# A two-layer attention kernel: the scores of a head pair as two 64-row matmuls into two banks

## The reference, cut to what matters

```python
# layer A: differential attention, 6 pairs of heads (c = 0, 1), causal
s = einsum('bqhcd,bkhcd->bhcqk', qi, kf) * scale
s = where(kpos <= qpos, s, NEG)
p = softmax(s); w = p[:, :, 0] - lam * p[:, :, 1]
o = einsum('bhqk,bkhe->bqhe', w, vf)            # then an RMS norm
# both layers: attention to a memory of 256 tokens, 4 heads, no mask
# layer B: 12 heads; with 256 tokens it is plain causal attention in one block
# third block, first half: 8 heads that share one key and one value,
#   the 64 best keys of each query (mask), a bias by distance, softmax
# third block, second half: retention, 8 heads: (q k^T * decay) v, no softmax
```

## Time and profile before

| | us |
|---|---|
| runs before, lowest, median, highest | 988.36, 989.8, 990.0 |
| profiled execution, its own time | 988.6 |
| its span in the trace | 986.9 |
| TensorE busy | 947.6 (96%) |
| VectorE busy | 570.8 (58%) |
| ScalarE busy | 474.7 (48%) |
| GpSimd busy | 70.9 (7%) |

### The profile page before, as it was taken

The page is one execution under the profiler, slowest core; times in us unless marked ns, Lnnn a source line. Parts: engine busy times, 40 slices in busy tenths (PEclk is TensorE's granted clock), DMA queues, the critical chain, the costliest instruction groups (busy, mean ns, idle before and its releaser), DMA issues.

```text
span 986.9 us, 13015 instructions
## 1 busy us (share of the span) xinstructions
PE 947.6 (96%) x4630; PEld 789.8 (80%) x4630; DVE 570.8 (58%) x769; ACT 474.7 (48%) x699; POOL 70.9 (7%) x132
## 2 busy tenths in 40 slices
PE   5999989999999999899999999999897999999998
PEld 4788778888888887788888888888776888888887
DVE  3777756654555577453855545548887364544543
ACT  4766565534444365562744344446344454434341
POOL 2101120100000010001100000002133000000000
PEclk9999999999999999899999999999997999999999
DMA  8843234755555544221855556455422055656551
GB/s 286 290 138 129 87 105 134 254 190 176 199 178 172 169 166 133 86 86 44 272 178 199 180 179 199 138 174 184 155 91 76 27 165 187 200 174 194 187 170 43
DMA packets 95435, 157.77 MB, mean 160 GB/s; under 512 B 5928, under 2 KB 37624, under 8 KB 95392
## 3 DMA queue, kind: packets, MB, share of 16 engines
q1 hardware_dynamic: 93872, 155.09, 47.2%
q10 hardware_dynamic: 1488, 2.10, 0.7%
q0 software_dynamic: 32, 0.02, 0.0%
HBM read 156.12 MB, written 1.06 MB: 159 GB/s over the span
## 4 chain that ended last, share of the span: by engine, by line
PE 85%; DVE 6%; ACT 4%; POOL 2%; issue 2%; DMA 1%; SPq 0%; ACTq 0%; DVEq 0%; POOLq 0%
PE proj L1388 14%; PE proj L1390 13%; PE proj L1389 13%; PE outp L1388 6%; PE outp L1390 6%; PE outp L1389 6%; PE score L1388 5%; PE score L1390 5%; PE score L1389 5%; PE turn L1415 4%; PE score L1544 2%; PE outp L1589 2%; DVE wlo L1660 1%; ACT whi L1180 1%; ACT qk L1292 1%
## 5 line engine op out<-in xcount | busy, mean ns | idle before, releaser
L1660 DVE TENSOR_TENSOR wlo<-raw,whi 128x2048 fp32r<-128x2048 f32 x145 | 329.7, 2278 | 223.6 <-ACT whi L1186 147.9
L1388 PE MATMUL proj<-whi,set_hi 128*128 128x512 f32 (+1 forms) x656 | 262.5, 400 | 9.6 <-DVE wlo L1660 6.7
L1390 PE MATMUL proj<-whi,set_lo 128*128 128x512 f32 (+1 forms) x656 | 256.6, 391 | 0.0
L1389 PE MATMUL proj<-wlo,set_hi 128*128 128x512 f32 (+1 forms) x656 | 256.1, 390 | 0.0
L1186 ACT ACTIVATE whi<-raw 128x2048 fp32r<-128x2048 f32 x64 | 122.6, 1916 | 143.7 <-PE outp L1390 57.5
L1180 ACT ACTIVATE whi<-raw 128x2048 fp32r<-128x2048 f32 (+1 forms) x81 | 153.0, 1902 | 35.4 <-PE outp L1390 17.5
L1388 PEld LDWEIGHTS proj<-whi,set_hi 128*128 128x128 f32 x656 | 124.6, 190 | 35.1 <-issue 8.9
L1390 PEld LDWEIGHTS proj<-whi,set_lo 128*128 128x128 f32 x656 | 124.5, 190 | 26.4
L1389 PEld LDWEIGHTS proj<-wlo,set_hi 128*128 128x128 f32 x656 | 124.9, 190 | 23.8
L1388 PE MATMUL outp<-whi,set_hi 128*128 128x512 f32 x268 | 105.5, 394 | 0.1
L1390 PE MATMUL outp<-whi,set_lo 128*128 128x512 f32 x268 | 104.5, 390 | 0.0
(11 more groups left out here) (184 smaller groups left out, 931.4 us busy)
## 6 DMA issues: line engine op xcount, KB each, us to landing
raw<-in_a_w_up SPq DMA_DIRECT2D x32, 512.0 KB, 4.4
raw<-in_a_w_down SPq DMA_DIRECT2D x32, 512.0 KB, 4.4
raw<-in_b_w_up SPq DMA_DIRECT2D x32, 512.0 KB, 4.3
raw<-in_b_w_down SPq DMA_DIRECT2D x32, 512.0 KB, 4.4
raw<-in_w_gate SPq DMA_DIRECT2D x22, 512.0 KB, 4.0
raw<-in_w_up SPq DMA_DIRECT2D x22, 512.0 KB, 4.9
raw<-in_w_down SPq DMA_DIRECT2D x22, 512.0 KB, 3.8
raw<-in_a_w_in SPq DMA_DIRECT2D x20, 512.0 KB, 6.5
```

What stands on the lines that cost most here:

```text
L1388: pe.matmul(out_, hi, wh, start=start, stop=False)
L1389: pe.matmul(out_, hi, wl, start=False, stop=False)
L1390: return pe.matmul(out_, lo, wh, start=False, stop=stop)
L1660: dve.tensor_tensor(shaped(wlo, u), shaped(raw, u), shaped(whi, u), ALU.subtract).then_inc(lo_done, 1)
```

## The change

- Queries stay in pairs: `heads` goes, every `turn_heads` of queries uses `pairs`. The first memset on GpSimd covers blocks 8 to 11 only (for the index scores), the second is dropped, with one of the waits of ScalarE.
- Scores run over 64 partitions: head 0 on partitions 0 to 63 into bank `Sb[0]`, head 1 on 64 to 127 into `Sb[1]`. One step now has two items; item 0 lies at column 0 of both banks, item 1 behind it.
- The masks are written first. The causal mask becomes a block of three times 128 columns (triangle, zeros, triangle), one matmul of 384 columns for each bank. Bias and selection matmuls also come ahead of the scores.
- VectorE waits for both banks, takes both maxima; ScalarE waits for both items' maxima, then does the four exponentials. Both banks are freed together by the second item (`both_s`).
- Retention scores the same way, both `a` in one go.

```diff
...
+        cmask = sb("cmask", [P, 3, P], BF16)
...
-        headq = qk[:, 0:16, :].rearrange("p (b c) n -> p b c n", c=2)
...
+        pb = lambda n: ctx.enter_context(nc.psum_tensor(n, [P, 2, COLS], F32))
+        Pp, Tp, Sp, Op = pb("proj"), pb("turn"), pb("score"), pb("outp")
+        Pb, Tb, Sb, Ob = ([pair[:, i, :] for i in range(2)] for pair in (Pp, Tp, Sp, Op))
...
+        def both_s(release):
+
+            n = count.s
+            count.s += 2
+            f = [free["S", b] for b in range(2)]
+            free["S", 0] = free["S", 1] = release
+            return n, f
...
-            it.s, it.s_free = s_use((exp_done, it.exp + 1))
             ITEMS.append(it)
-            st = add("scores")
-            st.it = it
+            if len(ITEMS) % 2 == 0:
+                first = ITEMS[-2]
+                first.at, it.at = 0, first.n
+                st = add("scores")
+                st.items = [first, it]
+                st.s, st.s_free = both_s((exp_done, it.exp + 1))
             return it
...
-        qk_pieces = lambda a: heads(0, a, 2) + pairs(2, 16 + a, 2)
+        qk_pieces = lambda a: pairs(0, a, 2) + pairs(2, 16 + a, 2)
...
+                    for b in (0, 2):
+                        ins = pool.affine_select(out=cmask[:, b, :], in_=cmask[:, b, :], compare_op=ALU.is_ge, fill=NEG,
+                                                 base=0, pattern=[[-1, P]], channel_multiplier=1)
+                    ins.then_inc(consts_made, 1)
...
-                    pool.memset(qk[:, 0:16, :], 0.0).then_inc(heads_zeroed, 1)
+                    pool.memset(qk[:, 8:12, :], 0.0).then_inc(heads_zeroed, 1)
...
-                elif st.kind == "late_loads":
-                    pool.wait_ge(o_evac, st.o)
-                    pool.memset(qk[:, 0:16, :], 0.0).then_inc(heads_zeroed, 1)
...
+                    act.wait_ge(nmax_done, st.items[1].i + 1)
+                    for it in st.items:
...
+                        for c in range(2):
+                            dst = e[:, it.buf, c * it.n:(c + 1) * it.n]
+                            src = Sb[c][:, it.at:it.at + it.n]
+                            ins = act.activation(dst, src, ACT.Exp, bias=it.nm[:, c:c + 1], scale=SCALE,
+                                                 accum_out=it.rs[:, c:c + 1])
+                        ins.then_inc(exp_done, 1)
...
+                    if kind in ("diff", "causal"):
+                        for c in range(2):
+                            add_mask(c, Sb[c][:, 0:3 * P], identb[:], cmask[:, :, :].rearrange("p b n -> p (b n)"))
+                    for it in st.items:
+                        for c in range(2):
+                            S = Sb[c][:, it.at:it.at + it.n]
+                            if kind == "idx":
+
+                                c0 = P - P * it.t
+                                add_mask(c, S, flip[:], btoep[it.pair // 2][:, 2 * it.pair % 4 + c, c0:c0 + it.n])
+                                add_mask(c, S, identb[:], selmask[:, it.t, 0:it.n])
+                    for i, it in enumerate(st.items):
+                        for c in range(2):
+                            ins = pe.matmul(Sb[c][:, it.at:it.at + it.n], qk[HALF[c], it.q, tok(it.t)],
+                                            it.k[HALF[c], 0:it.n], start=not opened[c], stop=i == 1)
+                            opened[c] = True
+                            if i == 1:
+                                ins.then_inc(s_full, 1)
...
+                    for a in range(2):
                         for c in range(2):
+                            ins = pe.matmul(Sb[c][:, a * TOK:a * P + TOK], qk[HALF[c], 4 + st.p, tok(a)],
+                                            qk[HALF[c], Q_QB + st.p, a * P:TOK], start=a == 0, stop=a == 1)
+                            if a == 1:
+                                ins.then_inc(s_full, 1)
...
+                    dve.wait_ge(s_full, st.s + 2)
+                    for it in st.items:
+                        behind(dve.tensor_reduce(it.nm, Sp[:, :, it.at:it.at + it.n], AX_X, ALU.max))
+                        dve.tensor_scalar(it.nm, it.nm, -SCALE, None, ALU.mult)\
+                           .then_inc(nmax_done, 1)
...
+                    dve.wait_ge(s_full, st.s + 2)
+                    dve.wait_ge(*st.after)
+                    for a in range(2):
...
+                            dst, src = rt[:, a, o:o + n], Sb[c][:, a * TOK:a * TOK + n]
```

More of the change, by code:

```diff
@@ L359, in turn_heads @@
             return st.use
-        LOW, HIGH, ALL = slice(0, DH), slice(DH, P), slice(0, P)
+        HALF, ALL = [slice(0, DH), slice(DH, P)], slice(0, P)
         tok = lambda t: slice(t * P, (t + 1) * P)
@@ L535, in build @@
         d = [diff_item(0, 0), diff_item(0, 1)]
-        qm_use = turn_heads(zq[:, 0], [0, 1], heads(0, 6, 2), chunk_ready(ev.chunk))[-1]
+        qm_use = turn_heads(zq[:, 0], [0, 1], pairs(0, 6, 2), chunk_ready(ev.chunk))[-1]
         zfree[0] = qm_use + 1
@@ L709, in build @@
         m += [mem_item(1, 0, qm_use, mkB), mem_item(1, 1, qm_use, mkB)]
-        q_use = turn_heads(zq[:, 0], [0, 1, 2, 3], heads(0, 0, 4), rope_ready(r0_.rope))[-1]
+        q_use = turn_heads(zq[:, 0], [0, 1, 2, 3], pairs(0, 0, 4), rope_ready(r0_.rope))[-1]
         zfree[0] = q_use + 1
@@ L803, in retention_scores @@
             st = add("retention_scores")
-            st.p, st.use, st.banks, st.after = p, max(kb_use, qb_use), [], after
-            for a in range(2):
-                count.decayed += 1
-                st.banks.append(s_use((decayed, count.decayed)))
+            st.p, st.use, st.after = p, max(kb_use, qb_use), after
+            count.decayed += 2
+            st.s, st.s_free = both_s((decayed, count.decayed))
         def retention_out(p):
@@ L839, in build @@
         i1 = index_scores(1)
-        kb_use = turn_heads(zq[:, 1], [0, 1, 2, 3], heads(0, 4, 4), rope_ready(rk.rope))[-1]
+        kb_use = turn_heads(zq[:, 1], [0, 1, 2, 3], pairs(0, 4, 4), rope_ready(rk.rope))[-1]
         zfree[1] = kb_use + 1
@@ L881, in build @@
         tile(gb, 1, 0, xb)
-        qa_use = turn_heads(zq[:, 0], [0, 1, 2, 3], heads(0, 0, 4), lambda t: (qn_done, t + 1))[-1]
+        qa_use = turn_heads(zq[:, 0], [0, 1, 2, 3], pairs(0, 0, 4), lambda t: (qn_done, t + 1))[-1]
         zfree[0] = qa_use + 1
@@ L1534, in _ @@
                 elif st.kind == "scores":
-                    it = st.it
-                    wait_turned(it.need)
-                    wait(it.s_free)
-                    if it.kind == "idx":
-                        pe.wait_ge(sel_done, it.t + 1)
-                        pe.wait_ge(bias_landed, 32)
-                    S = Sb[it.s % 2]
-                    for c in range(2):
-                        o = c * it.n
-                        ins = pe.matmul(S[:, o:o + it.n], headq[:, it.q, c, tok(it.t)], it.k[:, 0:it.n],
-                                        start=True, stop=it.kind == "mem")
-                        if it.kind == "idx":
-                            c0 = P - P * it.t
-                            pe.matmul(S[:, o:o + it.n], flip[:], btoep[it.pair // 2][:, 2 * it.pair % 4 + c, c0:c0 + it.n],
-                                      start=False, stop=False)
-                            ins = pe.matmul(S[:, o:o + it.n], identb[:], selmask[:, it.t, 0:it.n],
-                                            start=False, stop=True)
-                        elif it.kind != "mem":
-                            ins = pe.matmul(S[:, o + it.n - P:o + it.n], identb[:], cmask[:], start=False, stop=True)
@@ L1555, in _, with add_mask @@
-                    ins.then_inc(s_full, 1)
+                    wait_turned(max(it.need for it in st.items))
+                    for c in range(2):
+                        wait(st.s_free[c])
+                    kind = st.items[0].kind
+                    if kind == "idx":
+                        pe.wait_ge(sel_done, st.items[0].t + 1)
+                        pe.wait_ge(bias_landed, 32)
+                    opened = [False, False]
+                    def add_mask(c, dst, lhs, rhs):
+                        pe.matmul(dst, lhs, rhs, start=not opened[c], stop=False)
+                        opened[c] = True
```

53 lines of the change are left out of this document (11 added, 42 removed).

## The result

| | us |
|---|---|
| before, median of 11 runs (lowest, highest) | 989.19 (988.05, 990.2) |
| after, median of 11 runs (lowest, highest) | 992.24 (990.41, 995.89) |
| ratio after to before, 95% interval | 1.0040 [1.0027, 1.0052] |
| profiled execution of after: its own time, its span | 995.89, 994.2 |

The kernel became 3 us slower. The profiled execution of after is the slowest of its eleven: 3.7 us above their median. Its trace therefore shows some of the loss larger than it usually is.

What follows compares the result with a forecast made beforehand. TensorE, busy 947.6 of 986.9 us, was taken as the bound, with latency counting in exposed steps. Gains of 3.3 us against delays of 7.1 made it net 3.8 us slower: 993.5 us, range 986 to 1000.

Steps and rivals of the forecast that it cites:

- the delays in my sum: Later hand-over in exposed diff, causal, last idx and retention steps: 7.1 us paid, 2.7 of it in three causal steps.
- my gains: Shorter TensorE parts in covered diff, mem, causal and idx steps, plus cheaper query copies: 3.3 us kept.
- the signs that I had named: Trace checks: idle time up 5 to 7 us, busy time down; wrong if clock-0.50 time changes by more than 3 us.
- The wait of the 434.49 kind: TensorE's wait before the second item's transposes in a causal step: to grow from 0.47 to 0.9 us.
- TensorE's part of a step: TensorE time per step: diff and causal 1.50 us, gain about 0.2; mem 1.37 us, gain 0.36.
- Five slots for eight passes: Score matmuls as two tiles overlap partly: 0.87 us against 1.30 in diff or causal steps, 1.08 against 1.73 in mem.
- Rival 1: Passes overlap to one half and changing tile size is free: 3.2 us faster, 986.6; 0.25, shared with a removed clock stretch.
- The change of tile size: Switching TensorE between 128-row and 64-row tiles costs 0.14 us a change, 0.29 in and out of a step.
- Latency of both items in one hand-over: In a causal step, first exponential at +3.0 us instead of +1.48, last transposes at +4.8 instead of +3.91.
- The copies: Full-height query copies save 7.7 us on ScalarE, mostly hidden; credited 0.8 at the third diff step, 0.25 before 396.97.
- rival 3: Half-clock stretches: one more costs about 2 us, one removed gains 3.4; no chance of its own, split between other cases.
- Where a product covers the hand-over: Steps with more TensorE work between scores and transposes than the delay: it costs nothing and the gain stays.

Runs made afterwards that it cites:

- the ladder: Four kernels compared: before with hand-over of both items 1006.99 us; after with full-height scores and half-height copies 1002.34; after with half-height copies 999.06; after 992.24.
- hand-over alone: Kernel before, with only VectorE waiting for both items' scores and ScalarE for both items' maxima: 1006.99 us, ratio 1.0189 to before.
- tiles in covered steps: Kernel before, with 64-row tiles, masks first and hand-over of both items only in steps that a whole weight product follows: 986.18 us, ratio 0.9974 to before.
- The fillers: Identity matmuls put into TensorE's waits: on the kernel after 990.09 us, ratio 1.0006 to before; on the kernel before 986.63 us, ratio 0.9977.

## Why the prediction was right, and which steps of it were wrong

The forecast was 993.5 us, slower; the median is 992.2, inside the range and on the forecast's side. The mechanism was the right one: the late hand-over costs more than the tiles give. That the sum came out is luck all the same. By the ladder, full-height scores and half-height copies with the late hand-over, masks first and the banks by head cost 13.3 us, where the delays in my sum were 7.1; tiles and copies then gave back 10.1, where my gains were 3.3. Two misses of 6 to 7 us cancelled.

Of the signs that I had named, some came out against me. The time at clock 0.50 changed by 27 us in the profiled execution, where more than 3 was to mean wrong. TensorE's busy time rose by 5.3 us, by the half clock, instead of falling, and its idle time grew by 2.0 us (39.3 to 41.3) and not by 5 to 7. The wait of the 434.49 kind stayed at 0.47 us and didn't grow to 0.9; the new one of 0.91 came as named. The transposes did come later, and the step stayed above 1.2 us.


- **TensorE's part of a step** was mis-sized. "Five slots for eight passes" assumed that a matmul of tile B can't start beside the first pass of tile A. The pairs start 6 to 7 ns apart, so it is four slots: a differential step takes 1.29 us instead of the 1.50 forecast, a memory step with its entry 1.15 instead of 1.37. Rival 1's full overlap was true. The Trainium skill (TensorE: Matmul & The Clock Gate, Part 3: Packing small matmuls — row/col tiling) has starts about 4 ns apart, and the trace agrees in kind with 6 to 7.
- **The change of tile size** was about right. The two masks start at 60.031 and 60.205 and the first tile pass at 60.460, so after a mask of 0.17 it comes 0.08 late, and this first pass lasts 0.21 us (to 60.674) where the next of the same width lasts 0.11. Behind the last pass, at 61.010, the next work starts 0.31 us later, of which the pass itself takes 0.21: 0.10, and its first transpose takes 0.05 more than those behind it (61.317, 61.481, 61.590). That is 0.18 in and 0.15 out, where I had 0.14 each way. Rival 1's free change didn't come.
- **Latency of both items in one hand-over** was right in the trace: first exponential +2.87 us (forecast +3.0), last transposes +4.64 (+4.8). The diff stretch cost +3.5 us with 3.4 at half clock in it (forecast +2.3), the product behind the idx steps waited 1.9 us for its score bank, where it had waited 0.40 at 775.79. Not foreseen was the rotation on VectorE behind the maxima, 1.16 us at 90.41.
- **The price of that hand-over as a whole** was far too low: 7.1 us of delays in my sum, where hand-over alone cost 18, and with masks first and the banks by head 13.
- **The copies** failed most clearly. I credited 1.05 us; half-height copies in after cost 6.8. By the ratios it is 5.2, and still five times my term. My step "Most of it is hidden beside products" was the wrong one: the copies cost spread over most stretches, 2.2 us before 115.85 without any half clock. The stretch of the second layer's query turns fell by 4.3 us, where I had 0.25, but that is for the most part not the copies: with half-height copies and tiles in covered steps it fell by 3.7. There the place of the half clock counts. That a shorter wait "may remove" the stretch of 6.8 us stood only among the rivals; it came halfway, since 3.4 us came back at 388.9.
- **The clock** was in my text only as rival 3, with "one more stretch of a few us, about 2 us" at 434 to 446. In the profiled execution that place held 13.6 us at half clock, and all of the trace 27 us more than before. The fillers put its part of the median at about 2 of 3 us, an estimate. A correct forecast should have carried it in every delay of an exposed step, not beside the sum.
- **Where a product covers the hand-over**, the gains should have stayed. The kernel with tiles in covered steps alone was 3.0 us faster, near its 3.6, but its trace has the gain in the query turns and not in those steps, so this isn't shown. What I had left out is that a VectorE or ScalarE result further on is then waited for (0.55 us at 72.94, 0.49 at 90.16).

## What to carry to other kernels

When heads run as tiles into one bank each, hand over by bank and not by item: the maxima of head 0 for all items, then its exponentials beside the maxima of head 1. In this kernel that made a 0.4% loss a 0.6% gain. A delay on a TensorE that waits for it should be priced together with the stretch at half clock that may follow. Where one stretch of a trace gained a lot, look first whether its half clock has moved: here such a stretch looks like a gain of the copies in one kernel and of the tiles in another. Compare runs of equal granted clock before a gain of 2 or 3 us is put down to an edit. Tiles with a late hand-over did no harm where a weight product follows; that they gain there remains to be shown.

## What the hardware did that I had not expected

- Two 64-row tiles of fp32 matmuls, two passes each, ran wholly side by side, their records 6 to 7 ns apart; only the first pass of such a group took 0.21 us where the next of its width took 0.11. With the heads issued one behind the other they still did so, 13 ns apart; work of one tile passed earlier issued work of the other.
- Small waits went with long stretches, by one profiled execution each: two waits of 0.91 and 0.47 us in each 5.13 us went with 10.2 us at half clock, one of 0.77 in 4.54 with none.
- Fillers of identity matmuls in waits made the kernel before 2.4 us faster, for no work of use. On the kernel with the hand-over by bank they halved the time at half clock of the profiled execution and moved the median by less than can be told; why, stays open.
